# Token halves as the stationary operand in w_out and w_down, with the two halves' PSUM banks alternating

## The reference, cut to what matters

```python
h = _rmsnorm(x, norm_mix)
b, c, xt, v = split(h @ w_in)                       # 2048 -> 4 x 1024
y_conv = b * causal_depthwise_conv3(c * xt)
y_pool = pool_scale * per_group_linear(trailing_mean(v) - v)
x = x + concat(y_conv, y_pool) @ w_out              # 2048 -> 2048
h = _rmsnorm(x, norm_mlp)
x = x + relu(h @ w_up)**2 @ w_down                  # 2048 -> 8192 -> 2048
return _rmsnorm(x, norm_final)
```

## Time and profile before

| | us |
|---|---|
| median of 3 runs | 1023.91 |
| lowest and highest | 1023.52, 1024.41 |
| span of the profiled execution | 1023.5 |
| PE busy (share) | 1006.3 (98%) |
| PE weight loads busy | 873.4 (85%) |
| DVE busy | 628.1 (61%) |
| ACT busy | 440.5 (43%) |
| HBM read | 187.77 MB, mean 186 GB/s |

### The profile page before, as it was taken

One profiled execution on the slowest core, in us unless ns is written; L12 is line 12 of the kernel. 1 busy time (PEld: TensorE's weight loads), 2 busy tenths in 40 slices (PEclk: granted clock), 3 DMA queues, 4 the chain that ended last, 5 costly groups with the idle time before them and its releaser, 6 DMA issues.

```text
span 1023.5 us, 13766 instructions
## 1 busy us (share of the span) xinstructions
PE 1006.3 (98%) x5696; PEld 873.4 (85%) x5696; DVE 628.1 (61%) x453; ACT 440.5 (43%) x336; POOL 0.7 (0%) x8
## 2 busy tenths in 40 slices
PE   8999999999999999999999999999999999999994
PEld 7888888888888888888888888888888888888883
DVE  6797767666566666454666645465665455656555
ACT  6645344444444344434344433344353434344452
POOL 0000000000000000000000000000000000000000
PEclk9999999999999999999999999999999999999998
DMA  8846444445543645545454455454545545454502
GB/s 322 316 177 255 166 165 165 165 171 208 210 188 138 236 165 206 193 176 200 173 203 164 180 194 201 171 198 175 194 164 204 187 183 194 175 200 170 175 32 83
DMA packets 29264, 190.35 MB, mean 186 GB/s; under 512 B 3248, under 2 KB 3504, under 8 KB 7088
## 3 DMA queue, kind: packets, MB, share of 16 engines
q1 hardware_dynamic: 28944, 188.76, 50.1%
q10 hardware_dynamic: 288, 1.12, 0.3%
HBM read 187.77 MB, written 2.10 MB: 186 GB/s over the span
## 4 chain that ended last, share of the span: by engine, by line
PE 98%; DVE 1%; DMA 1%; ACT 0%; SPq 0%; issue 0%; DVEq 0%; ACTq 0%
PE ps L226 65%; PE ps L228 31%; PE ps L225 2%; DMA w_raw<-w_stream 1%; DVE x L865 0%; DVE inv_rms L613 0%; PE ps L264 0%; SPq L184 0%; PE ps L352 0%; DVE w_lo L630 0%; ACT w_hi L420 0%; DVEq L76 0%; DVE inv_rms L618 0%; DVE val L849 0%; DVE win L616 0%
## 5 line engine op out<-in xcount | busy, mean ns | idle before, releaser
L226 PE MATMUL ps<-act_a,w_hi 128*128 128x512 f32 x1536 | 541.8, 399 | 2.7 <-DVE w_lo L630 2.7
L544 DVE TENSOR_TENSOR w_lo<-w_raw,w_hi 128x2048 fp32r<-128x2048 f32 x172 | 391.6, 2290 | 236.2 <-ACT w_hi L365 234.3
L365 ACT ACTIVATE w_hi<-w_raw 128x2048 fp32r<-128x2048 f32 x172 | 326.3, 1912 | 291.0 <-PE ps L228 283.1
L226 PE MATMUL ps<-act_b,w_hi 128*128 128x512 f32 x1280 | 450.9, 398 | 0.0
L228 PE MATMUL ps<-act_a,w_lo 128*128 128x256 f32 x1440 | 404.4, 281 | 0.0
L226 PEld LDWEIGHTS ps<-act_a,w_hi 128*128 128x128 f32 x1536 | 287.4, 188 | 72.3 <-DVE w_lo L630 3.2
L228 PE MATMUL ps<-act_b,w_lo 128*128 128x256 f32 x1200 | 337.1, 281 | 0.0
L226 PEld LDWEIGHTS ps<-act_b,w_hi 128*128 128x128 f32 x1280 | 239.3, 188 | 57.5
L228 PEld LDWEIGHTS ps<-act_a,w_lo 128*128 128x128 f32 x1440 | 272.1, 189 | 1.0
L228 PEld LDWEIGHTS ps<-act_b,w_lo 128*128 128x128 f32 x1200 | 226.7, 189 | 1.0
L551 DVE TENSOR_TENSOR val<-ps,cross 128x1024 f32<-128x1024 f32 x45 | 55.1, 1223 | 94.6 <-ACT cross L371 94.6
(11 more groups left out here) (62 smaller groups left out, 170.7 us busy)
## 6 DMA issues: line engine op xcount, KB each, us to landing
w_raw<-w_stream SPq DMA_DIRECT2D x172, 1024.0 KB, 4.8
w_raw<-w_stream SPq DMA_DIRECT2D x16, 256.0 KB, 8.5
out<-x SPq DMA_DIRECT2D x8, 256.0 KB, 2.4
x<-x_t SPq DMA_DIRECT2D x3, 512.0 KB, 8.6
c_mem<-pool_w ACTq DMA_DIRECT2D x1, 1024.0 KB, 9.3
x<-x_t SPq DMA_DIRECT2D x1, 384.0 KB, 4.8
x<-x_t SPq DMA_DIRECT2D x1, 128.0 KB, 2.5
prm<-params ACTq DMA_DIRECT2D x1, 72.0 KB, 2.7
```

Of the source, the lines that this page charges most:

```text
L226: mm = pe.matmul(ps[:, bank, :], weights_hi, act, start=first, stop=last)
L365: act.activation(w_hi[:, c, :], w_raw[:, c, :], ACT.Copy).then_inc(hi_ready, 1)
L544: dve.tensor_tensor(out=w_lo[:, c, :], in0=w_raw[:, c, :], in1=w_hi[:, c, :].bitcast(F32), op=ALU.subtract)\
```

## The change

In w_out and w_down (20 of the 44 blocks) the roles of the operands are exchanged. The stationary operand is now 128 features x 128 tokens of `act_b` (hi or lo part, token half t = 0 or 1), the moving one is the 512 output columns of `w_hi` or `w_lo` of a block. For one k this makes six matmuls of 512 columns: hi·w_hi for t = 0, 1, lo·w_hi for t = 0, 1, hi·w_lo for t = 0, 1, each half with its own bank, so that consecutive matmuls always write to different banks (`row_products`). The output now stands with tokens on the partitions, already added up over the three products in one bank.

What follows from that layout:

- `x` is kept by rows (128 tokens x 2 halves x 2048) and is loaded a second time in that form (`x_rows`, 2 MB); the feature layout of the input (`x_feat`) is only used for the first norm's scaling. It lies in the memory of v and u now, so that the pool weights' load waits until it is used.
- ACT's copy and DVE's two additions per w_out or w_down block become one addition of DVE, PSUM to `x` (`add_rows`).
- w_up needs features on the partitions again: PE turns each new quarter of x with 8 transposes (`turn_x`, 32 in all), placed behind the first chunk of the following block; ACT and DVE make `act_a` from PSUM.
- Sums of squares are taken along the row by ACT (`accum_out`), the factor of a token is worked out on 128 x 2 values, and for the first two norms PE spreads it over the partitions through a diagonal matrix (`spread_norm`).
- The last block is computed one token half after the other; the first half is normalised and stored beside PE's work on the second.

`w_in`, `w_up` and the pool jobs are computed as before.

The diff at its core:

```diff
+        def turned_tile(j, i):
+            at = S * (i % 2)
+            return ps[:, NT * (j % 2) + 2 + i // 2, at:at + S]
+        def row_banks(parity):
+            return ps[:, NT * parity:NT * parity + HALVES, :]
+        def x_cols(j):
+            return x[:, :, BLOCK_COLS * j:BLOCK_COLS * (j + 1)]
...
+            load_chunk(1, 0)
+            load_chunk(1, 1)
+            for t in range(HALVES):
+                sp.dma_start(x[:, t, :], x_rows[:, t, :]).then_inc(x_rows_loaded[t], 16)
+            load_chunk(1, 2)
+            load_chunk(1, 3)
...
+            def spread_norm(r):
+                pe.wait_ge(diag_ready, HALVES * (r + 1))
+                for t in range(HALVES):
+                    mm = pe.matmul(ps[:, 0, P * t:P * (t + 1)], ones[:, :], diag[:, t, :],
+                                   start=True, stop=True)
+                mm.then_inc(spread, 1)
+            def turn_x(j):
+                pe.wait_ge(summed, turn(FIRST_OUT + j) + 1)
+                if j >= 2:
+                    pe.wait_ge(act_ready, 4 + (j - 1))
+                for i in range(NT):
+                    for t in range(HALVES):
+                        at = BLOCK_COLS * j + P * i
+                        mm = pe.transpose(turned_tile(j, i)[:, P * t:P * (t + 1)],
+                                          x[:, t, at:at + P], prm[:, IDENT:IDENT + P])
+                mm.then_inc(turned, 1)
+            def row_products(c, k, parity, halves=range(HALVES)):
+                a = act_b[:, CK * c + k, :]
+                at = BLOCK_COLS * k
+                hi_cols = w_hi[:, c, at:at + BLOCK_COLS]
+                lo_cols = w_lo[:, c, at:at + BLOCK_COLS]
+                first, last = c == 0 and k == 0, c == CHUNKS - 1 and k == CK - 1
+                for i, (of_act, cols) in enumerate(((0, hi_cols), (S, hi_cols), (0, lo_cols))):
+                    for t in halves:
+                        at = of_act + P * t
+                        mm = pe.matmul(ps[:, NT * parity + t, :], a[:, at:at + P], cols,
+                                       start=first and i == 0, stop=last and i == 2)
+                return mm
+            def row_block(n, parity, acts_before, turn_after=None):
+                pe.wait_ge(summed, turn(n) - 1)
+                for c in range(CHUNKS):
+                    pe.wait_ge(act_ready, acts_before + (c + 1))
+                    pe.wait_ge(lo_ready, 4 * n + (c + 1))
+                    for k in range(CK):
+                        mm = row_products(c, k, parity)
+                    mm.then_inc(chunk_used, 1)
+                    if turn_after is not None and c == 0:
+                        turn_x(turn_after)
...
-            with pe.Fori(0, 2) as i:
-                gemm_block(2 * i + FIRST_OUT, act_b, 0, 0)
-                gemm_block(2 * i + (FIRST_OUT + 1), act_b, 1, 0)
-            gemm_block(FIRST_UP, act_a, 0, 4)
+            for j in range(OUT_BLOCKS):
+                row_block(FIRST_OUT + j, j % 2, 0, turn_after=j - 1 if j else None)
+            pe.wait_ge(act_ready, 4 + 3)
+            gemm_block(FIRST_UP, act_a, 0, 4, turn_after=3)
...
             def down_pair(n, acts_before):
-                gemm_block(n, act_b, 0, acts_before)
-                gemm_block(n + 1, act_b, 1, acts_before)
+                row_block(n, 0, acts_before)
+                row_block(n + 1, 1, acts_before)
...
-            gemm_block(BLOCKS - 2, act_b, 0, 4 * PARTS + 4)
-            gemm_block(BLOCKS - 1, act_b, 1, 4 * PARTS + 4, chunks=(0, 1))
-            for nt in range(NT):
-                for c in (2, 3):
-                    if nt == 0:
+            row_block(BLOCKS - 2, 0, 4 * PARTS + 4)
+            pe.wait_ge(summed, turn(BLOCKS - 1) - 1)
+            for t in range(HALVES):
+                for c in range(CHUNKS):
+                    if t == 0:
                         pe.wait_ge(act_ready, 4 * PARTS + 4 + (c + 1))
                         pe.wait_ge(lo_ready, 4 * (BLOCKS - 1) + (c + 1))
                     for k in range(CK):
-                        mm = products(act_b, c, k, 1, (nt,))
-                mm.then_inc(last_tile_done, 1)
-            pe.wait_ge(summed, turn(BLOCKS - 2) + 1)
-            pe.wait_ge(last_added, NT - 1)
-            pe.matmul(ps[:, 0, 0:S], mean_of[:, :], squares[:, 0, :], start=True, stop=False)
-            pe.wait_ge(last_squared, NT)
-            pe.matmul(ps[:, 0, 0:S], mean_of[:, :], squares[:, 2 * NT - 1, :],
-                      start=False, stop=True).then_inc(mean_ready, 1)
...
+            def square_half(t, j, count):
+                act.wait_ge(ssq_ready, count - HALVES)
+                act.activation(junk(t), x[:, t, BLOCK_COLS * j:BLOCK_COLS * (j + 1)],
+                               ACT.Square, accum_out=ssq[:, t, j:j + 1]).then_inc(ssq_ready, 1)
...
+            for t in range(HALVES):
+                act.wait_ge(x_rows_loaded[t], 16)
+                act.activation(junk_wide(t), x[:, t, :], ACT.Square, accum_out=ssq[:, t, 0:1])\
+                   .then_inc(ssq_ready, 1)
             split(1, 2)
-            square(0, 2)
-            square(0, 3)
             split(1, 3)
+            root(0, 0, HALVES)
...
+                n = FIRST_OUT + 1 + j
+                for c in range(CHUNKS - 1):
+                    split(n, c)
+                act.wait_ge(summed, turn(n - 1) + 1)
+                square_rows(j, HALVES * (1 + j))
+                split(n, CHUNKS - 1)
+                act.wait_ge(turned, j + 1)
+                for i in range(NT):
+                    a = act.activation(act_a[:, NT * j + i, 0:S], turned_tile(j, i), ACT.Copy,
+                                       scale=col(G_MLP + NT * j + i))
+                a.then_inc(act_hi_ready, 1)
+            root(1, 0, HALVES)
...
+            for j in range(3):
+                act.wait_ge(summed, turn(BLOCKS - 4 + j) + 1)
+                square_rows(j, HALVES * (1 + OUT_BLOCKS + j))
+            for t in range(HALVES):
+                act.wait_ge(half_updated, t + 1)
+                square_half(t, 3, HALVES * (1 + OUT_BLOCKS + 3) + t + 1)
+                root(2 + t, t, t + 1)
+                act.wait_ge(r_ready, 2 + t + 1)
+                for j in range(2):
+                    xj = x[:, t, BLOCK_COLS * j:BLOCK_COLS * (j + 1)]
+                    act.activation(xj, xj, ACT.Copy, scale=r_tok[:, t:t + 1]).then_inc(out_by_act, 1)
...
+            def add_rows(n, parity, j):
+                dve.wait_ge(chunk_used, 4 * n + 4)
+                dve.tensor_tensor(out=x_cols(j), in0=row_banks(parity), in1=x_cols(j), op=ALU.add)\
+                   .then_inc(summed, 1)
+                dve.wait_ge(summed, turn(n) + 1)
+            def row_section(n, parity, j):
+                for c in range(CHUNKS - 1):
+                    split(n, c)
+                add_rows(n - 1, parity, j)
                 split(n, CHUNKS - 1)
...
+            def token_rms(r, t0, t1, sums):
+                mean, inv, tmp = tok_mean[:, t0:t1], tok_inv[:, t0:t1], tok_tmp[:, t0:t1]
                 def step(i, op):
                     op.then_inc(newton, 1)
                     dve.wait_ge(newton, 4 * r + i + 1)
-                step(0, dve.reciprocal(inv_rms[:, :], inv_rms[:, :]))
-                step(1, dve.scalar_tensor_tensor(out=tmp, in0=mean, scalar=EPS, in1=inv_rms[:, :],
-                                                 op0=ALU.add, op1=ALU.mult))
-                step(2, dve.tensor_tensor(out=tmp, in0=tmp, in1=inv_rms[:, :], op=ALU.mult))
+                dve.tensor_scalar(mean, sums, 1.0 / D, EPS, op0=ALU.mult, op1=ALU.add)\
+                   .then_inc(mean_ready, 1)
+                dve.wait_ge(root_ready, r + 1)
+                step(0, dve.reciprocal(inv, tok_root[:, t0:t1]))
+                step(1, dve.tensor_tensor(out=tmp, in0=mean, in1=inv, op=ALU.mult))
+                step(2, dve.tensor_tensor(out=tmp, in0=tmp, in1=inv, op=ALU.mult))
                 step(3, dve.tensor_scalar(tmp, tmp, -0.5, 1.5, op0=ALU.mult, op1=ALU.add))
-                dve.tensor_tensor(out=inv_rms[:, :], in0=inv_rms[:, :], in1=tmp, op=ALU.mult)\
-                   .then_inc(inv_rms_ready, 1)
-                dve.wait_ge(inv_rms_ready, r + 1)
+                dve.tensor_tensor(out=r_tok[:, t0:t1], in0=inv, in1=tmp, op=ALU.mult)\
+                   .then_inc(r_ready, 1)
+                dve.wait_ge(r_ready, r + 1)
+            def spread_rms(r):
+                token_rms(r, 0, HALVES, ssq[:, :, 0] if r == 0 else tok_sum)
+                for t in range(HALVES):
+                    dve.tensor_scalar(diag[:, t, :], prm[:, IDENT:IDENT + P], r_tok[:, t:t + 1], None,
+                                      op0=ALU.mult).then_inc(diag_ready, 1)
...
+            for t in range(HALVES):
+                xt = x[:, t, 3 * BLOCK_COLS:D]
+                dve.wait_ge(half_done, t + 1)
+                dve.tensor_tensor(out=xt, in0=ps[:, NT + t, :], in1=xt, op=ALU.add)\
+                   .then_inc(half_updated, 1)
```

(45 more changed lines are left out.)

323 lines of the change are left out of this document (139 added, 184 removed).

## The result

| | median us | runs |
|---|---|---|
| before | 1024.16 | 1023.52 to 1024.71 (4) |
| after | 1005.64 | 1005.23 to 1006.04 (4) |

The ratio is 0.982, with a 95% interval from 0.9806 to 0.9834: 18.5 us faster, where the forecast 1016.6 would have been 7.6. The time lies in the stated range, but the gain is more than twice the forecast one.

What follows compares the result with a forecast made beforehand. PE's matmul stream was taken as the bound. Row blocks -7.4, transposes +5.8, norms' matmuls +0.3, start +0.5 and tail -6.5 sum to -7.3 us on a 1023.5 span; with 0.4 to the median, 1016.6, range 1003 to 1028.

Steps and rivals of the forecast that it cites:

- What bounds the kernel: Whole kernel: PE's stream of matmuls is the time, PE busy for 98% of the span; DVE and ACT savings worth nothing.
- The row blocks: The 20 w_out and w_down blocks: 0.2315 us per 512-column matmul, 22.22 us a block instead of 22.59, -7.4 us.
- a block under 21.8: Sign in w_out and w_down: the forecast of 22.2 us a block is wrong if one takes under 21.8.
- The first rival: w_out and w_down: longer streams pay more, 0.225 us per 512-column matmul, -19.8 us, total 1004.2; chance 18%.
- The banks: PE's stream: 512 columns cost 0.2353 us before a matmul on the same bank, less (0.2315 or 0.225) before another bank.
- The transposes: 32 new ones between chunks of PE's stream, 0.18 us each judged by plain float32 matmuls, no waiting: +5.8 us.
- The norms' matmuls: PE's norm work: two means of 0.24 us go, four spreads of 128 columns at 0.18 come: +0.3 us.
- The start: Block 1: second input load delays chunk 2 to 42.0, wanted at 42.4, just fits; +0.5 us, bounds 0 and 3.
- The tail: Behind PE's last product: 14.6 us shrinks to 8.1 through a shorter closing chain, -6.5 us, bounds -5 and -7.
- Span against median: Whole kernel: the median of the runs was put 0.4 us above the profiled execution's span of 1023.5.

Runs made afterwards that it cites:

- m2: New kernel, PE alone: fp32r matmuls of 512 and 256 columns alternating or grouped, bf16, plain float32; alternating took 0.3533 us a pair, groups of 16 took 0.3479.
- m1: New kernel, PE alone: streams of 96 fp32r matmuls, varying widths, banks and operands; 512 columns took 0.2267 us each, 256 took 0.1200, an alternating pair 0.3533.
- e1: Changed kernel, with each k's three products of one token half first, so two of three consecutive matmuls write to the same bank: 1005.73 us.
- e8: Changed kernel, with the last block done whole, both token halves in turn and reported together at its end: 1009.58 us.
- e10: Changed kernel, with each of the 32 transposes of x done twice in a row: 1009.3 us.

## Why the prediction was wrong

- **What bounds the kernel** was right: PE's stream, its clock unchanged.
- **The row blocks** are the step that failed, as a size: -7.4 us forecast, -16.6 measured. The sign "a block under 21.8" came in. The mechanism as I put it, 512 columns cheaper behind 512, was half right. The term was a distance of 0.2315 taken from the pool jobs; a stream of 512s has 0.2267. In the pool jobs only two matmuls of 512 stand together, between ones of 256, and their single starts in the trace before are indeed 0.232 apart. But that is the price behind a change of size, where the first five are slow (m2), and not that of a stream. I had also divided a pair by its columns into 0.2353 + 0.1177, where the parts alone are 0.2267 and 0.1200 (m1): each fp32r matmul of 256 or 512 columns pays 13 ns beside its columns. "Six of 512, again 3072, so by columns nothing is gained" passed over the 32 matmuls fewer: 32 x 0.0134 = 0.43 us of a block's 0.83. The other 0.40 is the loss from mixed sizes, 64 x (0.3530 - 0.3467).
- **The first rival**, 0.225 from the change of a block with 18%, was nearest. That its 1004.2 lies so close is in part luck: it had the row blocks at -19.8 and the transposes at +5.8, two errors that go against each other.
- **The banks** had no part. I had read 0.2353 "to the same bank" against less "to another"; e1, m1 and m2 show no difference.
- **The transposes** cost +3.3, not +5.8. Plain float32 matmuls were the wrong neighbour: they leave two records each, a transpose here one (32 records for 32).
- **The norms' matmuls** were right: two spreads take 0.36 (from 47.84 to 48.20) where a mean took 0.24, +0.2 for both norms.
- **The start** was sized at +0.5, bounds 0 and 3, and cost nothing: chunk 2 was ready at 42.0, as forecast, and wanted at 42.3. The 42.0 is luck to the tenth: ACT's split ended at 39.7 instead of 39.2, and DVE's took 2.3 instead of 2.8. Of the 0.6 by which w_out began earlier, 0.4 are block 6, which the change doesn't touch.
- **The tail** was right as a sum, -6.5, and e8 shows 4 of it to be the halved last block. Its parts were not: the store behind the last scaling took 3.7 instead of 3.1, and the chain before it 4.4 instead of 5.0.
- **Span against median**: the forecast lay 11.0 above the measured median, 12.8 above the measured span. The median hides part of the error because the 0.4 from span to median was wrong, as said above.

## What to carry to other kernels

Count matmuls as well as columns: fp32r matmuls of 256 to 512 columns cost their columns plus some 13 ns each here, so fewer and wider ones gain even where the columns stay the same. Where two widths have to be mixed, sort them by width over a chunk; here that alone gave 13.3 us without touching a layout. Don't split the time of a pair by its columns, and don't take the price of a long stream from two matmuls between others: a pure stream of each kind, measured for a few microseconds, gives the two prices.

## What the runs showed of the hardware

- fp32r: 0.2267, 0.1743, 0.1200, 0.1111 us between starts at 512, 384, 256, 128 columns; bf16 0.2159, 0.1092, 0.0558 at 512, 256, 128.
- Whether consecutive matmuls share a bank or a moving operand, or load the same stationary tile again, made no difference above 0.5 ns at 512 columns (m1).
- Alternating 512 and 256 columns costs 6.6 ns a pair over the two pure streams in m1 and m2; groups of 2, 4, 8 and 16 cost 1.6, 4.1, 2.5 and 1.2 ns. In groups of 8 and 16 the first five 512s behind a 256 stand 228 to 236 ns apart, the later ones 227.
- The alternating order also ran without that loss, at 0.3468 us a pair over a whole block (block 6 of the changed kernel, 0.3530 before). What decides is open.
- A 128x128 transpose of plain float32 takes 0.10 us, one record, and lengthened the stream by 0.11 (e10); a plain float32 matmul of 128 columns 0.22, two records (m2).
